# Cross attention: fourth exponential and third probabilities ahead of the first output's parts; x turned over four banks; one border fewer

## The reference

```python
def memory_cross_attention(h, mem_n, wq, wkv, wo):      # 4 heads of 128 channels, 256 tokens, 256 memory rows
    q = (h @ wq).reshape(B, T, XA_HEADS, XA_DH)
    k, v = jnp.split(mem_n @ wkv, 2, axis=-1)
    ...
    s = jnp.einsum('bthd,bmhd->bhtm', q, k).astype(jnp.float32) * (XA_DH ** -0.5)
    p = jax.nn.softmax(s, axis=-1).astype(v.dtype)
    o = jnp.einsum('bhtm,bmhd->bthd', p, v).reshape(B, T, XA_W)
    return o @ wo

# first block
h = rms_norm(x, mix_norm_g[l])
p = h @ w_in[l]                                   # then three mixers: gated recurrence, mLSTM, attention
...
x = x + y @ w_out[l]
x = x + memory_cross_attention(rms_norm(x, xa_norm_g[l]), rms_norm(mem, mem_norm_g[l]), ...)
# second block, last lines of its second layer
y_lat = (o_lat * jax.nn.silu(g_l)) @ w_out        # 2048 x 2048, "mo" in the kernel
x = x + gate[:, None] * rms_norm_2(y_lat, post_norm[i])
```

## Time and profile before

| | us |
|---|---|
| median of 3 runs | 1780.98 (1780.79 to 1782.09) |
| profiled execution | 1781.63 |
| its span | 1779.8 |
| PE busy | 1701.5 (96%) |
| DVE busy | 1284.7 (72%) |
| ACT busy | 777.4 (44%) |
| TensorE's mean granted clock | 0.989 of full |

### The profile page before, as it was taken

How to read it: one execution, slowest core, us unless ns; L and a number is a source line. 1 busy time by engine, 2 the same in 40 slices (tenths; PEclk the granted TensorE clock), 3 DMA queues, 4 the chain that set the end, 5 groups by cost and what they waited for, 6 DMA issues and landing times.

```text
span 1779.8 us, 26263 instructions
## 1 busy us (share of the span) xinstructions
PE 1701.5 (96%) x10404; PEld 1473.5 (83%) x10404; DVE 1284.7 (72%) x2089; ACT 777.4 (44%) x1219; POOL 7.3 (0%) x14
## 2 busy tenths in 40 slices
PE   6999989999999799999999999999899989999897
PEld 6999989888988688888888878899897867777676
DVE  6899778487667688786887788776874756666544
ACT  6533384525456542332332233335544645454443
POOL 0000000000000000000000000000000000000000
PEclk9999999999999999999999999999999999999999
DMA  7788756547686353453555556562452463434353
GB/s 266 239 285 267 226 183 214 166 158 242 223 321 200 120 182 114 152 179 119 189 187 178 188 169 192 188 200 86 140 168 62 151 216 116 143 125 148 101 164 120
DMA packets 167699, 315.26 MB, mean 177 GB/s; under 512 B 14604, under 2 KB 22936, under 8 KB 167320
## 3 DMA queue, kind: packets, MB, share of 16 engines
q1 hardware_dynamic: 161152, 305.70, 52.8%
q10 hardware_dynamic: 5720, 5.78, 1.0%
q0 software_dynamic: 704, 2.10, 0.4%
HBM read 311.44 MB, written 2.10 MB: 176 GB/s over the span
## 4 chain that ended last, share of the span: by engine, by line
PE 61%; DVE 9%; ACT 3%; issue 1%; DMA 1%; ACTq 0%; DVEq 0%; SPq 0%
PE bank L598 15%; PE bank L599 15%; PE bank L600 15%; DVE w_low L352 3%; PE bank L3166 2%; PE bank L3167 2%; PE bank L3168 2%; PE bank L2894 1%; PE bank L2523 1%; PE bank L2895 1%; PE bank L2914 1%; ACT w_high L342 1%; DVE big L784 1%; PE bank L2905 1%; PE bank L2526 1%
## 5 line engine op out<-in xcount | busy, mean ns | idle before, releaser
L598 PE MATMUL bank<-operand,w_high 128*128 128x256 f32 (+2 forms) x2384 | 766.8, 322 | 37.4 <-DVE w_low L352 24.8
L599 PE MATMUL bank<-operand,w_high 128*128 128x256 f32 (+2 forms) x2384 | 753.1, 316 | 0.0
L600 PE MATMUL bank<-operand,w_low 128*128 128x256 f32 (+2 forms) x2384 | 752.7, 316 | 0.0
L342 ACT ACTIVATE w_high<-raw 128x1024 fp32r<-128x1024 f32 (+4 forms) x416 | 394.5, 980 | 422.6 <-PE bank L600 182.3
L352 DVE TENSOR_TENSOR w_low<-raw,w_high 128x1024 fp32r<-128x1024 f32 (+4 forms) x416 | 453.3, 1128 | 139.9 <-ACT w_high L342 137.3
L598 PEld LDWEIGHTS bank<-operand,w_high 128*128 128x128 f32 x2384 | 457.4, 192 | 86.9 <-issue 39.8
L599 PEld LDWEIGHTS bank<-operand,w_high 128*128 128x128 f32 x2384 | 457.7, 192 | 30.1 <-issue 2.4
L600 PEld LDWEIGHTS bank<-operand,w_low 128*128 128x128 f32 x2384 | 457.6, 192 | 27.9
L470 DVE SCALAR_TENSOR_TENSOR ada_acc<-ada_raw,silu_c,ada_acc 128x512 f32<-128x512 f32 x464 | 319.0, 746 | 10.0 <-DMA ada_raw<-in_ada_w 7.4
L598 PE MATMUL bank<-operand_small,w_high 128*128 128x512 f32 (+1 forms) x304 | 119.0, 392 | 7.1 <-DVE big L450 2.6
L600 PE MATMUL bank<-operand_small,w_low 128*128 128x512 f32 (+1 forms) x304 | 113.0, 372 | 0.0
(11 more groups left out here) (400 smaller groups left out, 1614.5 us busy)
## 6 DMA issues: line engine op xcount, KB each, us to landing
ada_raw<-in_ada_w SPq DMA_DIRECT2D x192, 512.0 KB, 4.2
raw<-in_w_in SPq DMA_DIRECT2D x96, 512.0 KB, 4.9
raw<-in_pool_w_in SPq DMA_DIRECT2D x64, 512.0 KB, 5.4
raw<-in_mla_w_in SPq DMA_DIRECT2D x48, 512.0 KB, 4.6
raw<-in_w_out SPq DMA_DIRECT2D x32, 512.0 KB, 5.9
raw<-in_pool_w_out SPq DMA_DIRECT2D x32, 512.0 KB, 5.7
raw<-in_mla_w_out SPq DMA_DIRECT2D x32, 512.0 KB, 4.6
raw<-in_xa_wkv SPq DMA_DIRECT2D x16, 512.0 KB, 4.6
```

Of the source, the lines that this page charges most:

```text
L342: ins = nc.scalar.activation(view(HI[:, slot, ks, :], False), view(RAW[:, slot, ks, :], True), ACT.Copy)
L598: pe.matmul(out_, hi, x[:, 0, :], start=first, stop=False, skip_group_check=True)
L599: pe.matmul(out_, hi, x[:, 1, :], start=False, stop=False, skip_group_check=True)
L600: return pe.matmul(out_, lo, x[:, 0, :], start=False, stop=last, skip_group_check=True)
```

## The change

It has three edits.

First, `front` no longer ends with `stage_end`. In its place ACT waits, before the first of its convolution taps, for DVE to have emptied the third tile of `win_b`. Other orders between the engines rest on the semaphores that are there.

Second, the order in cross attention: ACT runs `exponentials(3)` ahead of `high(0)`. DVE runs `probs(2)` ahead of `low(0)`, `probs(3)` ahead of `low(1)`, and the split of the first `xo` chunk moves from ahead of `probs(0)` to behind `probs(3)`.

Third, the pieces of x are turned into banks 4 to 7 in turn, so that PE waits only for the copy of the piece four before.

```diff
         def act_beside(act, c):
             s = nc.scalar.activation
             if c == 0:
+                act.wait_ge(dve_freed, win_b.free0 + 3)
                 for b in range(4):
                     act_lru_tap(act, b)
...
             turned(0)
             exponentials(2)
             turned(1)
+            exponentials(3)
             high(0)
-            exponentials(3)
             turned(2)
...
             maxima(0)
             maxima(1)
-            prime(dve, "cross", dve_low)
             probs(0)
             maxima(2)
             probs(1)
             maxima(3)
+            probs(2)
             low(0)
-            probs(2)
+            probs(3)
+            prime(dve, "cross", dve_low)
             low(1)
-            probs(3)
             low(2)
             low(3)
...
         def pe_turn_x(pe, n):
             k4, h, _ = piece(n)
-            if n:
-                xt_act.wait(pe, "c", n - 1)
+            if n >= 4:
+                xt_act.wait(pe, "c", n - 4)
             for m in range(4):
-                ins = pe.transpose(PB[4][:, m * P:(m + 1) * P], BIG[:, 4 * k4 + m, h * P:(h + 1) * P], ident[:, :])
+                ins = pe.transpose(PB[4 + n % 4][:, m * P:(m + 1) * P], BIG[:, 4 * k4 + m, h * P:(h + 1) * P], ident[:, :])
...
-                        xt_act.inc(s(XT[:, n % 2, piece(n)[2]], PB[4][:, :], ACT.Copy), "c", n)
+                        xt_act.inc(s(XT[:, n % 2, piece(n)[2]], PB[4 + n % 4][:, :], ACT.Copy), "c", n)
...
-                if name not in ("middle", "mixo","cross", "xo", "latents", "pairs", "mo"):
+                if name not in ("front", "middle", "mixo","cross", "xo", "latents", "pairs", "mo"):
                     stage_end(eng, me)
```

## The result

| us | before | after |
|---|---|---|
| median of the runs | 1782.26 (1780.79 to 1782.92, 6 runs) | 1770.61 (1768.38 to 1771.31, 6 runs) |
| profiled execution | 1781.63 | 1771.18 |
| its span | 1779.8 | 1769.4 |
| stretches at the lower clock, without the last one behind the work: number, us in all | 9, 34.1 | 8, 34.1 |

The ratio is 0.9932, 95% interval 0.992 to 0.9944. The forecast was 1769.7 us with a range of 1766.0 to 1774.2. The two profiled executions differ by 10.45 us. The forecast was taken from the first three runs of the kernel before (1780.98 us); over all six its median is 1782.26.

What follows compares the result with a forecast made beforehand. PE, busy 96% of the span, was taken as the bound, so only its waits could be won back. Gains of 3.0 + 5.1 + 3.3 = 11.4 us from the median 1780.98 gave 1769.6, stated as 1769.7 us, range 1766.0 to 1774.2.

Steps and rivals of the forecast that it cites:

- Border, 3.0 us: Between front and middle: ACT binds, starts its work 3.0 us earlier without the drain, and the kernel gains 3.0 us.
- The rival that takes PE's own 4.0 us: Border: PE binds, gaining 2.3 us of pause plus 1.7 us of slow clock; total 1768.6 us, chance 0.07.
- the low bound of 1.3 us: Border: the gain would be only 1.3 us if DVE's lead were what counts.
- Cross attention, 5.1 us: Cross attention: the new order ends `low(3)` at 592.2 instead of 597.3 us, gaining 5.1 us; bounds 3.4 and 6.7.
- hold of `high(0)` by 0.9 us: Cross attention: ACT's exponentials, moved ahead, hold `high(0)` 0.9 us after PE's output 0 is ready.
- The split on the path for about 1 us: Cross attention: PE waits for `low(1)`, behind DVE's moved split, so the split costs about 1 us.
- The slow spell that moves: Cross attention: a lower-clock stretch falls on output 3 or `xo`'s start, costing 1.6 us in all; 1771.3 us, chance 0.12.
- Turns, 3.3 us: Last product: two waits of PE before turns of x, 1.63 us each, vanish; gain 3.3 us, bounds 2.9 and 3.3.
- the margin of chunk 9: Last product: chunk 9's low part is finished 1.3 us before PE reaches it.
- The slower rival: Strips behind `xo`'s second chunk: PE waits for late weight units; at 30 us landing time 1784.7 us, chance 0.03.
- Given back: Stages behind cross attention: loads that don't start earlier take back gains, leaving 1774.7 to 1777.7 us; chance 0.06.
- the bounds 1767.0 and 1773.4: Whole kernel: totals from the sums of the high bounds (14.0 us gained) and the low bounds (7.6 us gained).

Runs made afterwards that it cites:

- PE freed: Kernel before, but PE neither drains nor waits at the border while ACT and DVE still meet and wait for PE's last chunk: 1782.45 us against 1781.42, ratio 1.0006.
- ACT freed: Kernel before, but ACT neither drains nor waits at the border, with the tap's wait added; PE and DVE still meet: 1778.85 us against 1781.42, ratio 0.9986.
- edit 2 alone: Kernel before with only the new order in cross attention on ACT and DVE: 1777.83 us against 1782.21, ratio 0.9966.
- edit 1: Kernel before with only the border change (`front` without `stage_end`, ACT's tap wait added): 1779.47 us against 1782.21, ratio 0.9988.
- edit 3: Kernel before with only the turns of x over four banks, waiting for the piece four before: 1777.75 us against 1782.21, ratio 0.9974.
- both turn variants: Kernel before with only x's turns changed: over four banks 1777.75 us (ratio 0.9974), over two banks 1778.78 us (ratio 0.9975), both against 1782.21.

## Why the prediction was right

The forecast of 1769.7 us stands 0.9 us below the measured median, and every term of its sum was found at its place. That the totals agree so well is in part luck: the base had risen by 1.3 us with three more runs of the kernel before, the medians differ by 11.65 us, and the profiled pair by 10.45. Point by point:

- **Border, 3.0 us.** Measured 2.99 us alone and 2.97 in the whole, counted from the last matmul of front (3.05 by the start of the same matmul). That ACT binds and not PE, which was argued from the wait of PE for ACT at 249 us and from ACT's list without idle time, is shown by the two runs that free one engine: PE freed gives 0, ACT freed gave 3.0 in an execution without a slow stretch behind PE's pause (with one, 1.5 by my estimate). The rival that takes PE's own 4.0 us is out. So is the low bound of 1.3 us: with DVE held as before the 3.0 us still came. The Trainium skill's rule (TensorE: Matmul & The Clock Gate, Part 1) that a throttled stretch costs its length times the missing share of the clock, 1.7 us for 3.4 us, comes close for PE's own matmuls here (1.49 us between the kernel before and edit 2 alone), but nothing of it reached the third chunk, where PE waited for DVE. In the account by place a stretch of 3.4 us that only one trace has shifts all that follows by 1.32, 1.56 and 1.62 us, and by 0.70 where a wait took part of it back.
- **Cross attention, 5.1 us.** In the profiled pair the first matmul of `xo` gained 8.34 - 3.28 = 5.06 us. The pieces: the forecast's hold of `high(0)` by 0.9 us was 0.96, of which 0.3 reach the end. The split on the path for about 1 us: the wait is 1.30 us and moving the split one place later is worth 1.44. The sum hit because the single durations were read from the rows and laid out anew, step by step. But it was worked out against one execution. The old order took 18.6 to 21.8 us in six traces, by how long its clock was low, and the new one 14.3 us in three: the edit is worth 4.3 to 7.5 us and 5.8 in the mean. That the clock makes the old order so unequal was not in the forecast, which counted the slow stretch as 1.3 us of one round.
- **The slow spell that moves** (chance 0.12). It came, in all traces with the changed order, but not onto output 3, and it cost 0.3 us at the start of `xo` (8.75 us instead of 8.44 for 60 matmuls). Of the rival's 1.6 us, 0.9 were for output 3 and did not come, and of the 1.7 us at `xo` the wait for DVE behind the first chunk took back more than the 1 us that was counted. The mechanism at `xo` was right, its chance too small and its price too high.
- **Turns, 3.3 us.** 3.24 us measured, at the two places, and the margin of chunk 9 was 1.2 us against 1.3.
- **The slower rival** (late units). Issued at 586.95 us, landed in at most 8.3 us, needed at 602.18 us: over 6 us in hand. The two units landed after 7.5 and 8.3 us, as before; the forecast's 6.7 to 8.3 us are those of units alone, the two raw halves issued with them took 3.7 and 6.7 us.
- **Given back.** No lead was lost to a load. What the profiled pair lost between 598 us and the last product, 0.95 us, is the net of slow stretches at other places and of three steps of about 0.3 us.

In the profiled pair the sum was 10.4 instead of 11.4 us. The missing 1.0 is 0.3 at `xo` and 0.95 for what lies between, less the 0.3 more that the lead had ahead of the cross attention. For such stretches the range had been widened, though not by the 1.7 us at each end that the text names: 1766.0 and 1774.2 lie 1.0 and 0.8 us beyond the bounds 1767.0 and 1773.4.

## What to carry to other kernels

When engines wait for each other at a barrier, ask for each one what it does next and which of them is without idle time until the next meeting: here only that engine's release shortened anything, and an experiment that frees one engine at a time shows it. Look then at how much wait the next engine has left; here it was none. A long block of work that is moved out of one engine's chain should be put where the next consumer doesn't stand behind it: one place later than it was put here was worth another 1.4 us. In a chain of short steps over three engines, price the change from several traces of before, since one execution can hold 0.8 us more than the best case and 2.5 less than the worst.

## What the runs showed of the hardware that was not expected

The totals of one kernel scatter by more than edit 1 or edit 3 moves them, and in the main with the clock. The same kernel had 1768.74 to 1773.89 us in five runs, with mean granted clocks of 0.992 and 0.988 at the ends; the kernel with edit 1 alone had spans of 1776.0 us at a mean clock of 0.991 and 1782.2 at 0.984, but also 1780.0 at 0.990, so the clock is not all of it. A slow stretch of 3.4 us that only one of two traces has is worth 1.3 to 1.6 us where PE is dense and has no wait behind it, 0.3 us at the start of `xo`, and nothing at the border.

At the border the pause of 2.4 us was followed by a slow stretch at 227 us in three of five traces (before, both turn variants) and not in the other two (cross alone, whose instructions there are the same, and ACT freed). So one trace doesn't tell whether a pause brings the lower clock.
